# The linear-attention mixer's program rewritten as ten steps a head, with gates and v leaving PSUM by ScalarE

## The reference

```python
proj = h @ w_in
q, k, v, g, lr = jnp.split(proj, ...)          # 4 heads: q, k 128 wide, v, g 256 wide; lr 2 x 16
def log_decay(lr_d, w2, bias):
    z = (lr_d @ w2 + bias).astype(jnp.float32)
    return jax.nn.log_sigmoid(z) / GLA_GATE_NORM
la_f = heads(log_decay(lr_f, w_gate2[0], b_gate[0]), GLA_DK)
la_b = heads(log_decay(lr_b, w_gate2[1], b_gate[1]), GLA_DK)
# o_i = sum_{j<=i} (q_i * exp(b_i - b_j)) . k_j v_j, b = cumsum(log_a); the backward one with j > i
o = (o_f + o_b).transpose(0, 2, 1, 3)
o = rms_norm(o, o_norm_g).reshape(B, S, GLA_V).astype(h.dtype) * jax.nn.silu(g)
return o @ w_out
```

## Time and profile before

| | |
|---|---|
| time, median of 3 runs | 2300.97 us (2299.47 to 2302.4) |
| the profiled execution's own time | 2295.68 us |
| its span | 2293.9 us |
| PE busy | 2239.7 us (98%) |
| DVE busy | 1270.2 us (55%) |
| ACT busy | 905.5 us (39%) |
| granted PE clock, mean | 0.994 |

### The profile page before, as it was taken

One profiled execution on the slowest core, in us unless ns is written; L12 is line 12 of the kernel. 1 busy time (PEld: TensorE's weight loads), 2 busy tenths in 40 slices (PEclk: granted clock), 3 DMA queues, 4 the chain that ended last, 5 costly groups with the idle time before them and its releaser, 6 DMA issues.

```text
span 2293.9 us, 24761 instructions
## 1 busy us (share of the span) xinstructions
PE 2239.7 (98%) x9874; PEld 1794.0 (78%) x9874; DVE 1270.2 (55%) x1970; ACT 905.5 (39%) x1402; POOL 154.3 (7%) x127
## 2 busy tenths in 40 slices
PE   7999999899899999999999999999899999999999
PEld 6888887766677888888888887777688888877777
DVE  6443445877754434455433445777566535655863
ACT  4222333555433322233322334777533222236672
POOL 2000002000040000020000012000040000020000
PEclk9999999999999999999999999999999999999999
DMA  5323224021123323223223224222045343331220
GB/s 188 101 83 110 97 69 149 19 92 56 35 78 127 114 92 110 83 100 112 83 83 128 78 69 145 72 72 90 19 129 165 120 138 114 103 129 52 77 74 37
DMA packets 201746, 217.39 MB, mean 95 GB/s; under 512 B 4968, under 2 KB 194536, under 8 KB 201632
## 3 DMA queue, kind: packets, MB, share of 16 engines
q1 hardware_dynamic: 194960, 193.48, 26.0%
q0 software_dynamic: 6528, 22.26, 2.9%
q10 hardware_dynamic: 144, 0.08, 0.0%
HBM read 213.66 MB, written 6.32 MB: 96 GB/s over the span
## 4 chain that ended last, share of the span: by engine, by line
PE 88%; DVE 6%; ACT 3%; issue 2%; DMA 0%; SPq 0%; DVEq 0%; ACTq 0%
PE ps L1581 87%; PE ps L1585 1%; DVE sb_wlo L1050 1%; ACT sb_whi L613 1%; DVE sb_gla_at L1302 1%; DVE sb_gla_ek L1287 1%; ACT sb_xh L613 0%; DMA sb_raw<-ffn_w_gu 0%; DVE sb_gla_eq L1290 0%; DVE sb_xl L1055 0%; DVE sb_gla_xb L1282 0%; DVE sb_gla_d L1269 0%; ACT sb_hyb_th L613 0%; DVE sb_gla_on L1213 0%; DVE sb_gla_vt L1196 0%
## 5 line engine op out<-in xcount | busy, mean ns | idle before, releaser
L1581 PE MATMUL ps<-sb_xh,sb_whi 128*128 128x512 f32 x2120 | 847.8, 400 | 22.7 <-DVE sb_xl L1055 10.3
L1581 PE MATMUL ps<-sb_xh,sb_wlo 128*128 128x512 f32 x2120 | 830.6, 392 | 0.0
L1581 PE MATMUL ps<-sb_xl,sb_whi 128*128 128x512 f32 x2120 | 829.9, 391 | 0.0
L1050 DVE TENSOR_TENSOR sb_wlo<-sb_raw,sb_whi 128x1024 fp32r<-128x1024 f32 (+2 forms) x401 | 474.1, 1187 | 517.2 <-ACT sb_whi L613 516.0
L613 ACT ACTIVATE sb_whi<-sb_raw 128x1024 fp32r<-128x1024 f32 (+2 forms) x401 | 387.0, 968 | 597.3 <-PE ps L1581 588.9
L1581 PEld LDWEIGHTS ps<-sb_xh,sb_whi 128*128 128x128 f32 x2120 | 401.1, 189 | 117.0 <-issue 25.1
L1581 PEld LDWEIGHTS ps<-sb_xl,sb_whi 128*128 128x128 f32 x2120 | 401.2, 189 | 86.6 <-issue 6.0
L1581 PEld LDWEIGHTS ps<-sb_xh,sb_wlo 128*128 128x128 f32 x2120 | 400.6, 189 | 85.6
L1581 PE MATMUL ps<-sb_ffn_ah,sb_whi 128*128 128x512 f32 x704 | 277.6, 394 | 0.0
L1581 PE MATMUL ps<-sb_ffn_ah,sb_wlo 128*128 128x512 f32 x704 | 276.0, 392 | 0.0
L1581 PE MATMUL ps<-sb_ffn_al,sb_whi 128*128 128x512 f32 x704 | 273.3, 388 | 0.0
(11 more groups left out here) (249 smaller groups left out, 1762.1 us busy)
## 6 DMA issues: line engine op xcount, KB each, us to landing
sb_raw<-ffn_w_gu SPq DMA_DIRECT2D x86, 1024.0 KB, 5.1
sb_raw<-ffn_w_down SPq DMA_DIRECT2D x32, 1024.0 KB, 4.9
sb_raw<-gla_w_in SPq DMA_DIRECT2D x12, 1024.0 KB, 5.3
sb_raw<-diff_w_in SPq DMA_DIRECT2D x12, 1024.0 KB, 5.1
sb_ada_raw<-w_ada POOLq DMA_DIRECT2D x12, 1024.0 KB, 6.2
sb_raw<-w_in SPq DMA_DIRECT2D x10, 1024.0 KB, 5.2
sb_raw<-ffn_w_down SPq DMA_DIRECT2D x16, 512.0 KB, 3.5
sb_raw<-ffn_w_down SPq DMA_DIRECT2D x16, 256.0 KB, 2.6
```

What stands on the lines that cost most here:

```text
L1050: e.tensor_tensor(lo, raw[panel % NRAW][:, 0:nk, off:off + 128], hi.bitcast(F32), ALU.subtract).then_inc(sem["w_lo"], 1)
L1581: return e.matmul(out, lhsT, rhs, start=start, stop=stop, skip_group_check=skip)
```

## The change

1. **The list.** Ten steps a head. In step t stand level t (DVE and ACT), one half or two, and then score product t (PE), one step behind its level. The matmuls of the next head's gates (`z`) stand behind score product 8, and the gates themselves behind score product 9. DVE's masked copy of product t-1 stands inside level t, behind `d1` and `d2`. ACT's copies of the two wide products are entries of their own (`copy`). The product with v is split in two entries (`pv`, one bank each, steps 3 and 6), the squares too (`osq`), and silu of G is moved to step 3 of the next head.
2. **Gates by ACT.** DVE's bias and min are gone. ACT reads z twice out of PSUM (Relu of -z-b, Abs of z+b), for both directions, then two Exp and two Ln, in two tiles (`z1` and `xb`) in place of one. DVE ends with one instruction for each direction and clears `xb`.
3. **Two row groups.** `lrs` and `w2` also lie on partitions 64 to 95, and the second direction's z matmul takes its operands from there. `w2` comes by two DMAs, and DVE writes `lrs` twice.
4. **v by ACT.** ACT copies v unscaled from PSUM to `gvt`. PE transposes it as before, and ACT's copy to `GV` becomes four of 128x128, each scaled by a column of `rbcol`. That is `rb` transposed: four transposes on PE and a small copy on ACT, once.
5. **Weights.** ACT makes `whi` three units ahead at a unit's first half, where nothing is waited for, and DVE `wlo` once a unit at the second half.

The core of the diff:

```diff
+    for tag in ("lr", "q"):
+        half(tag, 0, 0)
+        half(tag, 0, 1)
+    steps += [("rbT",), ("z", 0)]
+    half("k", 0, 0)
+    half("k", 0, 1)
+    steps.append(("gates", 0))
     for h in range(4):
+        units = [("q", h + 1), ("k", h + 1)] if h < 3 else []
+        units += [(tag, 2 * h + d) for tag in "vg" for d in range(2)]
+        halves = [(tag, i, k) for tag, i in units for k in range(2)]
+        for t in range(10):
+            if h and t == 0:
+                steps.append(("copy", h - 1, 9))
+            if t == 9:
+                steps.append(("copy", h, 8))
+            else:
+                steps.append(("level", h, t))
+            for _ in range(2 if h < 3 and t in (0, 5) else 1):
+                if halves:
+                    half(*halves.pop(0))
+            if h and t == 3:
+                steps += [("silu", h - 1), ("pv", h - 1, 0)]
+            if h and t == 6:
+                steps.append(("pv", h - 1, 1))
+            if h and t in (4, 7):
+                steps.append(("osq", h - 1, t // 7))
+            if h and t == 8:
+                steps.append(("oss", h - 1))
+            if h == 3 and t == 8:
+                steps += [("y", n) for n in range(4)]
+            if h == 3 and t == 9:
+                steps.append(("begin", 0, 4))
+            steps.append(("score", h, t))
+            if h < 3 and t == 8:
+                steps.append(("z", h + 1))
+            if h < 3 and t == 9:
+                steps.append(("gates", h + 1))
+            if h and t == 9:
+                steps.append(("on", h - 1))
...
 # ScalarE
+                        if half and tag == "v":
+                            used(w, u - 1)
+                            w.wait_ge(sem["g_vT"], i)
+                            act(gvt[:, :], psum[GLA_IN[g_unit[tag, i] % 2]][:, :], ACT.Copy).then_inc(sem["g_v"], 1)
+                    elif s[0] == "vT":
...
+                        for t in range(4):
+                            act(GV[n // 2 % 2][:, t, (n % 2) * 128:(n % 2 + 1) * 128],
+                                psum[GLA_MISC][:, t * 128:(t + 1) * 128], ACT.Copy,
+                                scale=rbcol[:, t:t + 1]).then_inc(sem["g_vrow"], 1)
+            def gates(h):
...
+                for d in range(2):
+                    b = ring_bank("z", h, d)
+                    w.wait_ge(sem["g_zmm"], 2 * h + d + 1)
...
+                    act((cf, ta)[d][:, :], b[:, :], ACT.Relu, scale=-1.0,
+                        bias=neg_b[:, d * 4 + h:d * 4 + h + 1]).then_inc(sem["g_zact"], 1)
+                    act((z1, xb)[d][:, :], b[:, :], ACT.Abs, bias=col("b_gate", d * 4 + h)).then_inc(sem["g_zact"], 1)
...
 # VectorE
+            def gates(h):
                 for d in range(2):
+                    out, z = (cf, ta)[d], (z1, xb)[d]
+                    w.wait_ge(sem["g_zact"], 8 * h + 7 + d)
+                    e.scalar_tensor_tensor(out=out[:, :], in0=out[:, :], scalar=-1.0, in1=z[:, :], op0=ALU.mult,
                                            op1=ALU.subtract).then_inc(sem["g_z"], 1)
+                w.wait_ge(sem["g_z"], 2 * h + 2)
                 e.memset(xb[:, :], 0.0).then_inc(sem["g_x0"], 1)
...
                 e.tensor_tensor(flat(d2), tf, half(xb, 0), ALU.subtract).then_inc(sem["g_dq"], 1)
+                if li:
+                    scores(h, li - 1)
...
 # TensorE
+                        for d, q in ((0, 96), (1, 64)):
+                            mm(ring_bank("z", h, d)[:, :], w2[q:q + 32, h * 128:(h + 1) * 128], lrs[q:q + 32, :],
+                               True, True).then_inc(sem["g_zmm"], 1)
```

More of the change, by code:

```diff
@@ L133, in hybrid @@
         self.out(w_out)
[L136 to L158, removed]
@@ L161, in gla_steps, with half @@
-def gla_steps():
-    steps = [("half", t, 0, half) for t in ("lr", "q", "k") for half in (0, 1)]
-    for h in range(4):
[L164 to L180, removed]
+def gla_steps():
+    steps, turn = [], [None]
+    def half(tag, i, k):
+        steps.append(("half", tag, i, k))
+        if turn[0] is not None:
+            steps.append(("vT", turn[0]))
+            turn[0] = None
+        if tag == "v" and k:
+            turn[0] = i
+    for tag in ("lr", "q"):
[5 more added lines that the diff above has]
+    steps.append(("gates", 0))
+    for h in range(4):
+        units = [("q", h + 1), ("k", h + 1)] if h < 3 else []
[30 more added lines that the diff above has]
+                steps.append(("on", h - 1))
+    steps += [("copy", 3, 9), ("silu", 3), ("y", 4), ("y", 5), ("begin", 1, 4), ("pv", 3, 0), ("pv", 3, 1), ("osq", 3, 0),
+              ("osq", 3, 1), ("more", 0, 6), ("more", 1, 6), ("oss", 3), ("on", 3), ("y", 6), ("y", 7), ("begin", 2, 6),
+              ("begin", 3, 6)]
@@ L409, in build @@
             G = t_("g", [128, 8, S])
[L410 removed]
+            w2 = t_("w2", [128, 512])
             mask = t_("mask", [128, 8, 128], I32)
@@ L527, in build, with ring_bank @@
         n_gate = rank(GATES)
+        g_ring = {}
+        for s in GS:
+            if s[0] == "z" or s[0] == "score":
+                for k in range(2 if s[0] == "z" or s[2] == 9 else 1):
+                    g_ring[s + (k,)] = len(g_ring)
+        def ring_bank(*key):
+            return psum[GLA_RING[g_ring[key] % 3]]
         rsqrt = [("norm", 0), ("norm", 1)]
-        rsqrt += [("g_o", s[1]) for s in GS if s[0] == "output" and s[2] == 2]
+        rsqrt += [("g_o", s[1]) for s in GS if s[0] == "oss"]
         rsqrt += [("norm", 2), ("norm", 3), ("norm", 4)]
@@ L1193, in gla @@
                             e.tensor_tensor(ks[i % 2][:, :], b[:, :], rb[:, :], ALU.mult).then_inc(sem["g_k"], 1)
[L1194 to L1196 removed]
                         else:
                             e.tensor_tensor(G[:, i, :], b[:, :], rb[:, :], ALU.mult).then_inc(sem["g_g"], 1)
[L1199 to L1207 removed]
+                    elif s[0] == "gates":
+                        gates(s[1])
+                    elif s[0] == "level":
+                        level(*s[1:])
+                    elif s[0] == "on":
                         h = s[1]
```

281 lines of the change are left out of this document (124 added, 157 removed).

## The result

| | before | after |
|---|---|---|
| median | 2300.22 us (2297.16 to 2302.4, 4 runs) | 2267.14 us (2263.01 to 2267.36, 4 runs) |
| profiled execution's own time | 2295.68 us | 2267.3 us |
| its span | 2293.9 us | 2265.5 us |
| the stage, from the first matmul of `lr` | 272.1 us | 241.8 us |
| granted clock, mean | 0.994 | 0.997 |

The ratio is 0.9852, with a 95% interval of 0.984 to 0.9865: the change makes the kernel 33 us faster. (The median of before was 2301.0 us over three runs when the forecast was made; the table has a fourth.)

A forecast was written before the change was run, and what follows sets the result against it. PE, busy 98% of the span, bounds the kernel. In the stage, work 240.7 + waits 1.2, 0.5, 3.2 + clock 1.7 = 247.3 us for 272.1, a gain of 24.8; forecast 2276 us, range 2268 to 2288.

The forecast's parts named there:

- B: Rival: each head's start is late all the same, with half clock behind the waits; 12.2 us more, 2288 us; chance 0.15.
- D: Rival: ACT's strict order makes every level late and the kernel slower, 2309 us at 3.2 us a level; chance 0.03.
- The step from the profiled execution to the median: Whole kernel: the profiled execution's 2270.9 us after the change, 5.3 us below the median, gives a median of 2276.2.
- half clock 8.5 us: Mixer's stage before: four stretches at half clock, 17.1 us, lose at most 8.5 us of PE's work.
- rival A: The forecast itself with its unknowns: best 2269 us, worst 2286; chance 0.77 together with the second row group doing nothing.
- z: 3.4 us saved, 1.7 forecast: Gate matmul pairs at heads' ends: only the middle two passes overlap, saving 0.4 us a head, 1.7 in all.
- The waits left: PE's remaining waits in the stage: 1.2 us at head 3's start, 0.5 for all heads, 3.2 for y.
- The head's start: From the end of z to `eq` of level 0: 12.2 us, with DVE's first `d` about 9 us behind z.
- PE's other work: PE's work in the stage at full clock: 241.9 us plus 0.5 for transposes less 1.7 for z, 240.7 after.
- The clock in the stage: One stretch of half clock is left, where PE waits for y near head 3's end, costing 1.7 us.
- ACT's four reads of PSUM: Gates at a head's start: four reads, each 0.583 us long, take 1.9 us together.
- The four scaled copies of a unit: ACT's 128x128 copies of v after its transposes: between 0.583 and 2.3 us together, taken as 1.0.

The follow-up runs named there:

- e1: The kernel before, unchanged, run again for the spread of its executions: 2301.07 us.
- e8: The kernel before with only the second direction's z matmul moved to the second row group: 2300.35 us.
- e2: The new list and weights alone, with gates and v on DVE as before and z in one row group: 2290.55 us.
- e3: The change with both z matmuls in one row group again: 2269.21 us.
- e5: The change with the gates done as before, DVE adding the bias: 2286.54 us.
- e12: The change with gates on DVE, both bias adds put in their own entry right behind z: 2273.55 us.
- e7: The kernel before with silu moved behind ACT's copies of the wide scores: 2288.37 us.
- e11: The change with ACT's gates done one direction after the other: 2265.33 us.
- e9: The change itself, unchanged, run again: 2266.65 us.
- e4: The change with begin of output unit 0 behind score product 9 of head 3, not ahead: 2264.33 us.
- e10: The change with begin of output unit 0 behind head 3's score product 9 and DVE's norm behind the next head's level 0: 2263.86 us.

## Why the prediction was wrong in its size

The direction, the mechanism and the order of the rivals were right: the waits for `vt` and `at` are gone, heads 1 and 2 run without a wait at full clock (B fails), no wait of PE in the stage is for ACT (D fails), and two waits are left where I put them. The size was off by 9.1 us, in these terms.

1. **The step from the profiled execution to the median: 5.5 us, the largest miss.** This is the step "it stands 5.3 us below the median of the runs, and the median becomes 2276.2". I made the sum against one execution and carried its distance from the median, 5.3 us, over to the changed kernel as if it were fixed. It was clock: the profiled execution of before had 0.994, the ordinary one 0.991 (e1), and a nearly equal kernel at 0.991 shows 27.3 us at half clock in the stage where I counted 17.1 (e8). By that trace the term "half clock 8.5 us" is up to 13.7 in an ordinary run. The changed kernel does not lose this: its runs are at 0.997 to 0.999, and its profiled execution stands 0.2 us above its median. Its few waits are not the whole reason, since the new order alone keeps 21.2 us of them and runs at 0.996 (e2). That the profiled execution of before lay 3.8 us below the fastest of its three runs could have told that it was a lucky one. The best case of rival A, 2269, goes by the same step, and so the range ended above the result.
2. **z: 3.4 us saved, 1.7 forecast.** I took the middle between two bounds, by an order of issue that I had argued and not seen. Pairs of 1.06 against 1.91 us (1.13 against 1.98 with the last pass's end, e3) show the upper bound. Here the Trainium skill, "TensorE: Matmul & The Clock Gate", "Why this matters for your kernels", was right where my number was not: by it the whole second matmul is saved, and it is. e8 adds a condition: its pair in head 0, back to back, overlaps, and its pairs in heads 1 to 3, with a wait of 1.8 us between, do not.
3. **The waits left: 2.8 us, 4.9 forecast** (y 2.0 for 3.2, `eq` at head 3 0.8 for 1.2, 0 for 0.5 elsewhere). The head's start was counted well: 12.0 us for 12.2, `d` at 8.9 for "about 9". For y I had added ACT's inverse root and exponentials one behind the other after the sums; 1.2 us of that was too much, and which part of it I have not taken apart.
4. **PE's other work: 1.7 us less than forecast.** 241.8 - 2.8 - 1.7 = 237.3 against 240.7, of which z is 1.7. Half of the other 1.7 is z again. In the stage z's busy time before and after is

```profile
L1581 PE MATMUL ps<-sb_gla_lrs,sb_gla_w 32*128 32x512 f32 x16 | 8.7, 633 | 5.4 <-ACT sb_gla_at L613 5.4
L1599 PE MATMUL ps<-sb_gla_lrs,sb_gla_w 32*128 32x512 f32 x16 | 4.5, 640 | 0.0
```

4.2 us less, not 3.4: parted by a wait, a pair takes 1.12 + 1.05 = 2.17 us, back to back 1.91 (e3), and three pairs were parted. So a stop of PE cost 0.26 us here beyond its idle time as the profile gives it, and the forecast had nothing for that. The last 0.9 us is not assigned. (The 8.5 us of clock in the sum was the most that it could be: in the last stretch of the earlier trace rows PE was idle for 1.7 of the 6.83 us, so PE's work before can be up to 0.9 higher, and as much more is unassigned.)
5. **Elsewhere: 1.9 us the other way.** The stage won 30.3 us and the span 28.4, mostly for the stretch of half clock near the start, which comes and goes in both kernels.

Together 5.5 + 1.7 + 2.1 + 1.7 - 1.9 = 9.1 us.

The clock in the stage came out at 1.7 us, as forecast, at the place that I named (y).

I costed ACT's four reads of PSUM by the row of a plain copy, 0.583 us; with a bias they take 0.681 to 0.697, but they start 0.57 to 0.58 apart (492.36 to 492.94), so the chain was right. The four scaled copies of a unit take 9.0 / 8 = 1.1 us of ACT together, 0.364 each since they overlap, inside the bounds of 0.583 and 2.3 and near the 1.0 that I took. On the rule that I set against the change (the Trainium skill, "ScalarE: Activation LUTs", "Rules for kernel authors": relu and add belong on VectorE): it did not decide. The gates on DVE made the kernel 19.4 us slower (e5) though one add takes 0.740 us and ACT's reads about as much; 13.0 of that was the place in DVE's queue (e12).

What the rewrite is worth, then: its order alone (with part 5, which has no run of its own) 8 to 10 us, the gates' way 19.4, v 2.6, the second row group 2 to 3, each measured by taking it back from the full change (the order by itself). They come to 32 to 35 for 33. The last three one by one, 24 to 25, agree with e2, which lacks all three and stands 23.4 above the change. Whether the gates' way would be worth as much in the old order was not run. The mere removal of silu from ACT's path at the head's end is worth 10 in the old order (e7), and the new list holds that too.

**What stays open.** Why one wait of 2 us is followed by half clock and the same wait in another kernel's execution is not: e11 has the wait for y of 2.0 us and no stretch behind it, the change and e9 have both; and behind the stage e4 and e10 have stretches behind waits that pass without one in the change and e9. Why the new order alone runs at 0.996 with as many us of waits as before, so how much of the clock that the change won is owed to its missing waits. And the 0.9 us of point 4.

## What to carry to other kernels

Before work is moved to another engine, look at what stands ahead of it in its queue: an instruction that waits for a long piece of PE's work holds everything behind it, and moving DVE's adds ahead of such an instruction (e12) bought 13.0 of the 19.4 us that a new engine bought, while moving one silu (e7) bought 10 in the old order. Sum against a typical run, not against the one that was profiled: compare its mean clock with that of the others first, and if it is higher, widen the range towards the faster side by the difference, which the change may win and may not. And where two matmuls of few rows lie in two row groups, as here, take the saving in full when they stand back to back, and at nothing when a wait stands between them.

## What the runs showed of the hardware

- Two fp32 matmuls with 32 rows of operands on partitions 96 to 127 and 64 to 95 take 1.06 us together, back to back; both on 96 to 127 take 1.91, and 2.17 with a wait between them (its 1.8 us not counted).
- A wait of PE of about 2 us costs more than itself where the clock falls behind it, which it did in some executions and not in others: stretches of 3.41 us at 0.50 began 0.65 and 0.67 us behind waits of 1.89 and 1.88 us (e7), and 1.35 us behind one of 2.05 (after). Removing 5.9 us of waits gave 10 (e7).
- The same program varied by 7 us (e1), and its mean granted clock by 0.004 with it. The changed kernel, with 2.8 us of waits, varied by 3 to 4 us at 0.997 to 0.999, and the new order alone, with 21.2 us, by 2 at 0.996 (e2): the sum of the waits does not give the clock.
- An instruction that waits holds its engine's queue: DVE's bias add behind an eviction that waited 4.89 us for PE (e5), put ahead of it, gave 13.0 us back (e12).
